# Reordering the joints of a Strassen-style feed-forward on one Trainium2 core: low parts and sums from GpSimd to VectorE, one early eviction, sums and adds at the tail placed anew

## What is computed

```python
x = x + rmsnorm(ox @ p['x_wo'], nrm[3])
h = rmsnorm(x, nrm[4])
u, fconv_new = causal_dwconv(h @ p['f_wu'], fconv, p['f_conv_w'], p['f_conv_b'])
x = x + rmsnorm((jax.nn.gelu(u) * (h @ p['f_wg'])) @ p['f_wd'], nrm[5])
```

## Time and profile before

| | us |
|---|---|
| median of 3 runs | 2322.34 (2321.3 to 2322.55) |
| the profiled execution, its time | 2326.86 |
| its span, first to last instruction | 2325.1 |
| PE busy in it | 2185.2 (94%) |
| DVE busy | 1285.1 (55%) |
| ACT busy | 845.4 (36%) |
| POOL busy | 631.3 (27%) |
| mean granted TensorE clock | 0.964 of full |

### The profile page before, as it was taken

How to read it: one execution, slowest core, us unless ns; L and a number is a source line. 1 busy time by engine, 2 the same in 40 slices (tenths; PEclk the granted TensorE clock), 3 DMA queues, 4 the chain that set the end, 5 groups by cost and what they waited for, 6 DMA issues and landing times. The chain is left out here.

```text
span 2325.1 us, 42807 instructions
## 1 busy us (share of the span) xinstructions
PE 2185.2 (94%) x17107; PEld 2003.3 (86%) x17107; DVE 1285.1 (55%) x2341; ACT 845.4 (36%) x1712; POOL 631.3 (27%) x518
## 2 busy tenths in 40 slices
PE   9999998988888989999899999987899999999996
PEld 7799977865555579999899988987899999999996
DVE  2213354356675761222237154566799887876958
ACT  4221244136655640111243133543333433334353
POOL 0000025502223121211011200235344333445535
PEclk9999999979999999999999999998899999999997
DMA  4211097964444321111310255232223232264243
GB/s 150 99 51 46 28 175 241 326 240 126 147 128 146 125 103 55 59 41 41 129 46 28 98 203 208 95 110 83 88 72 122 84 121 88 84 236 177 90 144 118
DMA packets 133713, 276.33 MB, mean 119 GB/s; under 512 B 24627, under 2 KB 79572, under 8 KB 128333
## 3 DMA queue, kind: packets, MB, share of 16 engines
q1 hardware_dynamic: 110796, 232.32, 30.1%
q0 software_dynamic: 10368, 28.33, 3.7%
q10 hardware_dynamic: 12352, 12.96, 1.7%
HBM read 229.49 MB, written 48.26 MB: 119 GB/s over the span
## 5 line engine op out<-in xcount | busy, mean ns | idle before, releaser
L88 PE MATMUL psum<-merged_high,oq_half 128*128 128x352 f32 x768 | 189.1, 326 | 9.3 <-DVE oq_half L69 7.7
L88 PE MATMUL psum<-ff_t,ff_x_slots 128*128 128x264 f32 x1200 | 149.1, 284 | 0.0
L88 PEld LDWEIGHTS psum<-ff_t,ff_x_slots 128*128 128x128 f32 x1200 | 147.1, 188 | 0.3 <-issue 0.2
L88 PEld LDWEIGHTS psum<-merged_high,oq_half 128*128 128x128 f32 x768 | 135.3, 190 | 9.9 <-DVE oq_half L69 8.0
L1655 POOL DMA_DIRECT2D na_kv<-in_pool x128 | 69.2, 540 | 226.3 <-PE psum L1859 154.9
L88 PE MATMUL psum<-x_half_high,mg_w_high 128*128 128x352 f32 x384 | 124.0, 323 | 2.1 <-ACT gated L2329 1.2
L88 PE MATMUL psum<-h_again_low,mg_w_high 128*128 128x352 f32 x384 | 123.1, 321 | 0.0
L88 PE MATMUL psum<-x_half_high,mg_w_low 128*128 128x352 f32 x384 | 123.1, 320 | 0.0
L1957 ACT ACTIVATE na_pt<-psum 128x512 f32<-128x512 f32 (+1 forms) x170 | 86.4, 543 | 89.1 <-PE psum L1832 80.6
L88 PE MATMUL psum<-ff_bslot,ff_x_slots 128*128 128x264 f32 x888 | 117.5, 285 | 0.0
L88 PEld LDWEIGHTS psum<-ff_bslot,ff_x_slots 128*128 128x128 f32 x888 | 112.4, 189 | 0.1
(11 more groups left out here) (667 smaller groups left out, 5662.9 us busy)
## 6 DMA issues: line engine op xcount, KB each, us to landing
na_kv<-in_pool SPq DMA_DIRECT2D x128, 128.0 KB, 3.8
na_kv<-in_pool POOLq DMA_DIRECT2D x128, 128.0 KB, 4.2
ff_bslot_raw<-mid_ops SPq DMA_DIRECT2D x59, 264.0 KB, 3.2
mid_ops<-ff_bufs SPq DMA_DIRECT2D x11, 1056.0 KB, 3.9
mg_w<-in_w_merge SPq DMA_DIRECT2D x15, 768.0 KB, 4.3
ring<-in_f_wu SPq DMA_DIRECT2D x11, 1024.0 KB, 5.2
low<-in_f_wg SPq DMA_DIRECT2D x22, 512.0 KB, 4.5
first_pages<-in_pool SPq DMA_DIRECT2D x68, 128.0 KB, 6.0
```

Of the source, the lines that this page charges most:

```text
L88: ins = nc.tensor.matmul(out, w[a], x[b], start=first and n == 0, stop=last and n == 2)
```

## The change

- GpSimd keeps the sum `t3,0` and the low part `b22,0`. The low parts `b22,1`, `t1,0`, `t4,0` and the sums `t3,1`, `t4,0` are now DVE's, at given places in its list.
- The eviction c11 of i = 2 comes before the low part `t3,1`; a semaphore of its own (`c11_early`) replaces its count, with `wait_c11` for its readers. u3 of 0 comes before c11 of 1, and the first weight sums of i = 1 before u4 of 0.
- In `pass1`, `spread(0)` moves from after step 2 to after step 1; `sums2(0)` and `(1)` from 8 to 9, `spread2(0)` from 9 to 10, `spread2(1)` from 11 to 12. DVE does `add_square(7, 2)` before the low part `b11,1`, the low part `b21,1` after the first `factor` of the third group, and both `add(3, ..)` before the `mean` of the second norm.
- The eleven differences of down weights for p = 3 are formed while the pieces for p = 4 are prepared.
- In the tail DVE does the residual adds of groups 0 and 1 right after their scales; POOL keeps group 2. `sums3(2)` comes after c = 1, j = 0 and `spread3(2)` after j = 2. DVE scales group 2 before the fourth part of group 3 is added.

The diff without the list of semaphore names (`c11_early` and `summed5` are added there):

```diff
@@ -3216,11 +3216,12 @@
         x_stored = [sem(f"x_stored{g}") for g in range(4)]
-        T_POOL, T_DVE = (("t3", 0), ("t3", 1), ("t4", 0)), (("t1", 0), ("t1", 1), ("t2", 0), ("t2", 1), ("t4", 1))
+        T_POOL, T_DVE = (("t3", 0),), (("t1", 0), ("t1", 1), ("t2", 0), ("t2", 1), ("t3", 1), ("t4", 0), ("t4", 1))
         HIGH_ORDER = [("b11", 0), ("b21", 0), ("b11", 1), ("b21", 1), ("b22", 0), ("t3", 0), ("b22", 1), ("t2", 0), ("t2", 1), ("t3", 1),
                       ("t1", 0), ("t1", 1), ("t4", 0), ("t4", 1)]
-        LOW_POOL = [("b22", 0), ("b22", 1), ("t1", 0), ("t4", 0)]
-        LOW_DVE = [("b11", 0), ("b21", 0), ("b11", 1), ("b21", 1), ("t2", 0), ("t2", 1), ("t3", 0), ("t3", 1), ("t1", 1), ("t4", 1)]
+        LOW_POOL = [("b22", 0)]
+        LOW_DVE = [("b11", 0), ("b21", 0), ("b11", 1), ("b21", 1), ("b22", 1), ("t2", 0), ("t2", 1), ("t3", 0), ("t3", 1), ("t1", 0), ("t1", 1),
+                   ("t4", 0), ("t4", 1)]
         block = ctx.enter_context(nc.Block())
@@ -3270,9 +3271,17 @@
 
+        def wait_c11(eng, i):
+            if i == 2:
+                eng.wait_ge(S["c11_early"], 1)
+            else:
+                eng.wait_ge(S["c11"], i + 1 if i < 2 else i)
+
         def wait_closed(eng, i, p):
...
                 eng.wait_ge(S["p3_kept" if p == 3 else "c22"], 1)
+            elif p == 2:
+                wait_c11(eng, i)
             else:
@@ -3328,7 +3337,7 @@
         WD_SUM = {}
-        for p, per in ((7, 1), (6, 2), (5, 0), (3, 1)):
+        for p, per in ((7, 1), (6, 2), (3, 1), (5, 0)):
             for q in range(KP):
@@ -3447,10 +3456,10 @@
                 for n, f in enumerate((0, 4) if g < 2 else (4, 0)):
-                    if g < 3:
+                    if g < 2:
                         sp.wait_ge(S["summed3"], 2 * g + n + 1)
                     else:
-                        sp.wait_ge(S["summed4"], n + 1)
+                        sp.wait_ge(S["summed5" if g == 2 else "summed4"], n + 1)
                     c = slice(f, f + 4)
@@ -3592,9 +3601,10 @@
                             ins.then_inc(S["z_done"], 1)
-                            if c == 1 and j == 1:
+                            if c == 1 and j == 0:
                                 sums3(2, 2 * down_pairs[0])
-                    spread3(2, 2 * down_pairs[1])
+                            elif c == 1 and j == 2:
+                                spread3(2, 2 * down_pairs[1])
                     return
@@ -3632,16 +3642,16 @@
                     sums(1)
-                elif t == 2:
+                elif t == 1:
                     spread(0)
...
                     spread(1)
-                elif t == 8:
+                elif t == 9:
                     sums2(0)
                     sums2(1)
-                elif t == 9:
+                elif t == 10:
                     spread2(0)
-                elif t == 11:
+                elif t == 12:
                     spread2(1)
@@ -3984,7 +3994,7 @@
                 w = xa[g // 2][:, ks, col(g % 2)]
-                nc.gpsimd.tensor_tensor(w, w, z[:, ks, col(g)], ALU.add).then_inc(S["summed3"], 1)
+                nc.gpsimd.tensor_tensor(w, w, z[:, ks, col(g)], ALU.add).then_inc(S["summed5"], 1)
 
@@ -3993,13 +4003,8 @@
             low_of(6)
-            operand_low("b22", 1)
-            t_sum("t3", 1)
             low_of(9)
             low_of(10)
-            operand_low("t1", 0)
-            t_sum("t4", 0)
-            operand_low("t4", 0)
             for n in range(11, ND):
@@ -4007,9 +4012,6 @@
                     low_of(down_at(pi, q))
-            for g in range(2):
-                for n, f in enumerate((0, 4)):
-                    add3(g, f, n)
             for n, f in enumerate((4, 0)):
@@ -4142,7 +4144,7 @@
                 elif what == "u2":
-                    ve.wait_ge(S["c11"], i + 1)
+                    wait_c11(ve, i)
                     ins = tt(cols(t12), src, cols(t12), ALU.add)
@@ -4162,11 +4164,14 @@
                     ins = tt(cols(t12), src, cols(t12), ALU.add)
-                ins.then_inc(S[what], 1)
+                ins.then_inc(S["c11_early" if (i, what) == (2, "c11") else what], 1)
 
...
                 m, h = int(what[1]) - 1, int(what[2]) - 1
-                ve.wait_ge(S["c" + what[1:]], 2 * q + 2)
+                if what == "m11":
+                    wait_c11(ve, 2 * q + 1)
+                else:
+                    ve.wait_ge(S["c" + what[1:]], 2 * q + 2)
                 ve.wait_ge(S["gelu_ready"], 2 * q + 2)
@@ -4242,8 +4247,7 @@
                 elif p == 3:
-                    wait_low(ve, down_at(DP[6], q))
-                    ve.wait_ge(S["wd12"], 16)
+                    wait_low(ve, down_at(DP[2], q))
                     ve.wait_ge(S["wd_sum"], WD_SUM[(6, q)])
@@ -4295,6 +4299,13 @@
                 nc.vector.tensor_scalar(rstd[0:TW, 2, c], psum[0:TW, at_bank, c], 1.0 / D, EPS, ALU.mult, ALU.add).then_inc(S["mean3_ready"], 1)
+
+            def add3(g, f, n):
+                ks = slice(f, f + 4)
+                ve.wait_ge(S["scaled3"], 2 * g + n + 1)
+                ve.wait_ge(x_again[g // 2], 16)
+                w = xa[g // 2][:, ks, col(g % 2)]
+                tt(w, w, z[:, ks, col(g)], ALU.add).then_inc(S["summed3" if g < 2 else "summed4"], 1)
 
@@ -4340,12 +4351,12 @@
             add_square(6, 2)
+            add_square(7, 2)
             operand_low("b11", 1)
-            operand_low("b21", 1)
-            add_square(7, 2)
             mean(SUM, 0, third, "sum_ready", 3, "mean_ready")
...
             factor(0, third, "root_ready", 2, "rstd_ready")
+            operand_low("b21", 1)
             scale(2)
@@ -4355,10 +4366,10 @@
             scale(3)
+            add(3, 0)
+            add(3, 1)
             mean(SUM2, 1, third, "sum2_ready", 3, "mean2_ready")
-            add(3, 0)
             factor(1, third, "root2_ready", 2, "rstd2_ready")
-            add(3, 1)
             normed(2, range(KD))
@@ -4366,26 +4377,31 @@
             t_sum("t1", 0)
+            operand_low("b22", 1)
             t_sum("t1", 1)
...
             operand_low("t2", 1)
+            t_sum("t3", 1)
             weight_low(0, 7)
             operand_low("t3", 0)
+            evac(2, "c11")
             operand_low("t3", 1)
+            operand_low("t1", 0)
             evac(0, "u2")
             operand_low("t1", 1)
+            t_sum("t4", 0)
             t_sum("t4", 1)
+            operand_low("t4", 0)
             operand_low("t4", 1)
+            evac(0, "u3")
             evac(1, "c11")
-            evac(2, "c11")
-            evac(0, "u3")
+            sums_early(1)
             evac(0, "u4")
...
             evac(0, "c22")
-            sums_early(1)
             evac(0, "c21")
@@ -4442,8 +4458,10 @@
                 for v in ahead:
-                    if DOWN_ORDER[v[0]] in (7, 6, 3):
+                    if DOWN_ORDER[v[0]] in (7, 6):
                         wd_sum(*v)
+                    elif DOWN_ORDER[v[0]] == 4:
+                        wd_sum(DP[3], v[1])
                 for i in range(max(len(ahead), len(drains))):
@@ -4452,18 +4470,23 @@
                 if p == 3 and b + 2 == len(blocks):
+                    ve.wait_ge(S["gained"], 8)
                     for g in range(2):
                         ve.wait_ge(S["row3_copied"], g + 1)
-                        ve.wait_ge(S["gained"], 8)
                         for f in (0, 4):
                             scale3(g, f, row3[:, g, :])
+                    for g in range(2):
+                        for n, f in enumerate((0, 4)):
+                            add3(g, f, n)
             for i in range(3):
                 add_square3(slice(0, HN))
-            def finish(c):
-                for j in range(4):
+            def finish(c, some):
+                for j in some:
                     z_add(3, j, c)
...
                         add_square3(col(c))
+                if 3 not in some:
+                    return
                 add_square3(col(c))
@@ -4472,20 +4495,17 @@
 
-            finish(0)
+            finish(0, range(4))
             factor(2, third, "root3_ready", 2, "rstd3_ready")
-            finish(1)
+            finish(1, range(3))
             scale_last(0, 4)
+            scale_last(0, 0)
+            finish(1, range(3, 4))
             factor(2, fourth, "root3_ready", 3, "rstd3_ready")
-            scale_last(0, 0)
             scale_last(1, 4)
...
             for n, f in enumerate((4, 0)):
-                ks = slice(f, f + 4)
-                ve.wait_ge(S["scaled3"], 7 + n)
-                ve.wait_ge(x_again[1], 16)
-                w = xa[1][:, ks, col(1)]
-                tt(w, w, z[:, ks, col(3)], ALU.add).then_inc(S["summed4"], 1)
+                add3(3, f, n)
 
...
 def build(nc, A, O):
```

4 lines of the change are left out of this document (2 added, 2 removed).

## The result

The changed kernel takes 2312.21 us (median of 9 runs, 2304.42 to 2318.68), the kernel before, on the same chip in the same session, 2325.11 (9 runs, 2321.3 to 2334.93). The ratio is 0.9929, 95% interval 0.991 to 0.9948: 12 to 21 us faster. The forecast of 2300.2 was 12.0 too low, and the time is above the range.

The account below looks back on a forecast made before the run. PE is full in the long products, so gains lie in its waits for DVE and POOL at the joints. 5.0 + 14.5 - 2.0 + 4.6 = 22.1 us off 2322.3 gives 2300.2, range 2294.8 to 2308.3 (some 80%).

Parts of the forecast that it names:

- Joint A: Norm passes, 1512 to 1564 us: earlier spreads and reordered DVE work gain 5.0 us, between 4.0 and 5.7.
- Joint B: Start of gate and up products, 1600 to 1647 us: five operations to DVE, c11 forward, gain 14.5 us (12.0 to 15.3).
- DVE chain: DVE's operations from the end of `normed(3)` to product (1,6), counted at 29.9 us; wrong if over 32.
- Rival 1: All PE waits vanish with nothing late next, B worth 21.3 us; time 2293; chance 4%.
- another length behind (1,6): Sign of being wrong: the stretch from product (1,6) to the down products not the same length as before.
- Joint C: Change of product in the down projection: eleven moved differences of down weights cost 2.0 us, between 0 and 5.0.
- second block: Where p=4 begins: 0.6 us added to the cost for the second block of three differences.
- rival 3: Differences alternate with POOL, fourth product stalls in several blocks, tail returns only 3 us: 2311 (2306 to 2317); chance 13%.
- Joint D: The tail, 2284 us on: residual adds on DVE, quarter sums and scales ahead, gain 4.6 us, between 3.0 and 6.5.
- So 23.0 to 23.5 instead of 21.5: Tail from `sums3(2)` to the end: longer than before's 21.5 us; 23.5 taken.
- I subtract the gain from the median: Step to the forecast time: gain reckoned in the profiled execution (2326.86 us), subtracted from the runs' median of 2322.34.
- Rivals 4 and 5: 4: another wait holds B's chain, about 2320, 5%; 5: DVE bounds the fourth product, half clock, 2324 to 2329, 3%.

Follow-up runs that it names:

- A alone: Kernel before with only the moved spreads and sums2, reordered squares, low part and adds of the norm passes: 2325.23 us, ratio 0.9986.
- C alone: Kernel before with only the eleven differences of down weights moved ahead of p=4: 2335.07 us in one run, beside 2331.85 before.
- D alone: Kernel before with only the tail changed (residual adds on DVE, quarter sums and scales ahead): 2324.01 us in one run, beside 2331.85 before.
- POOL held back: Changed kernel with POOL's group 2 adds after the last square and p=3 differences after the p=6 drains: 2304.77 us, ratio 0.9905.
- second set: The changed kernel again, no edit, against the kernel before: medians 2309.78 (6 runs) and 2327.88 us (23 runs), ratio 0.9922.
- C and D: Kernel before with both the moved differences of down weights and the changed tail: 2334.73 us in one run, beside 2331.85 before.

## Why the prediction was right or wrong

**Joint A, 5.0 (4.0 to 5.7): right.** `scale(0)` was to start 2.95 earlier. It stands 56.05 us into the stage against 60.09 before; 1.1 of those 4.0 is the clock of the first matmuls, since after a start at full clock the unchanged code has it at 58.9: 2.9. `normed(1)` starts 90.97 us into the stage instead of 96.86 (said: 4 us earlier). The tree's wait is gone, PE waits 2.68 at `sums(2)` ("about 3"), and DVE is what it waits for. `sums(2)` comes 7.1 us earlier than in the profile of before and 4.9 to 5.6 earlier than in the four executions of old code that began at full clock (101.45 to 102.15). With A alone (1,6) is 5.7 earlier than in before, 4.6 without the first 1.1. But by then the clock counts for more than A does: (1,6) stands 181.30 us into the stage with A alone, and 181.56 and 180.89 with C alone and D alone, which leave A's code as it was. The medians give A 0.2 to 6 us.

**Joint B, 14.5 (12.0 to 15.3): right, with one gain not seen.** At equal clock it is 14.57. The forecast's DVE chain was 29.9 us from the end of `normed(3)` to (1,6). The timeline of after:

```profile
1603.35 0.70 DVE L4145 TENSOR_TENSOR ff_bufs<-psum,ff_bufs 128x528 f32<-128x528 f32 x1
...
1611.80 3.15 PE L88 MATMUL psum<-ff_t,ff_slot_e 128*128 128x264 f32 x24 [1.08 <-DVE ff_t L69]
...
1616.43 6.12 PE L88 MATMUL psum<-ff_t,ff_slot_e 128*128 128x264 f32 x48 [1.48 <-DVE ff_bufs L4145]
...
1624.23 3.16 PE L88 MATMUL psum<-ff_t,ff_slot 128*128 128x264 f32 x24 [1.68 <-DVE ff_t L69]
...
1632.96 1.29 DVE L69 TENSOR_TENSOR ff_slot<-ff_slot_raw,ff_slot 128x512 fp32r<-128x512 f32 x2
...
1633.80 8.15 PE L88 MATMUL psum<-ff_t,ff_slot 128*128 128x264 f32 x48 [6.42 <-DVE ff_slot L69]
```

From 1603.35 to 1633.80 it is 30.45, with waits of 1.08, 1.48, 1.68 and 6.42 (said: 1.4, 1.9, 1.9 and 5). (1,6) stands 166.74 us into the stage, 20.2 earlier (said: 19.5, A and B together), and 19.1 without the 1.1 of the first matmuls. Rival 1, that all waits vanish, is out by the same row. What the forecast denied is the 2.0 us in stretch c: "after (1,6) the orders are the same", but DVE comes to the next products with less behind it, and two small waits there, 1.47 and 1.09, become one of 0.5. The forecast had named another length behind (1,6) as a sign of being wrong, and it came.

**Joint C, −2.0 (0 to −5.0): −2.7.** The term was 0.9 for each difference, less idle time, plus a second block. They took 1.73 each, and no second block stalled. 0.9 was drawn as a mean where the row has two prices and nothing between: of the eleven in the trace of before, eight take 0.68 to 0.69 us and three 1.78 to 1.80, and each of these three starts while a low part of POOL is under way, none of the eight does. The four that took 4.72 us together are two of either kind. So the bound from the earlier trace rows, 1.80, was the price to take beside a POOL that has work queued. The Trainium skill, "SBUF — State Buffer", section "Who interferes with whom", which has a VectorE operation with two SBUF inputs and a GpSimd operation that reads SBUF shut each other out, agrees with this row: 1.73 where 0.62 is the free price, and 0.70 as before for sums that read PSUM. Several blocks stalled, as rival 3 has it, did not come: d is 494.83 to 494.89 wherever the first three are away from the drains.

**Joint D, +4.6 (3.0 to 6.5): +1.7, the term that failed.** `sums3(2)` came 5.9 earlier in its stretch (said: 6.6); the four scales took 5.85 us (said: 4.9), the four adds 4.75 (4.9). PE waited 4.21 there (said: 2 to 4). The miss is behind it. "So 23.0 to 23.5 instead of 21.5" was 25.7: the working followed PE and DVE, and has no term for POOL's two adds of the third quarter. But `scale(2)`, moved ahead of the last squares, sets them free just there, and two squares took 3.92 us instead of 1.00. With POOL held back it is 22.7, a little better than said. The rule of the Trainium skill named at C bears on this place too, and the trace agrees with it; it had been weighed for C and B, and not for D.

**The sum inside the stage** is right by chance more than by its terms: 22.1 said, 21.3 measured. By stretches, 0.7 more than said up to (1,6) (0.4 less without the first matmuls' 1.1), 2.0 more in c, 0.7 less at C, 2.9 less at D. C and D together were to bring 2.6 and lost 1.0.

**The step that failed for the time** is "I subtract the gain from the median" of 2322.34. That was a median of three runs within 1.25 us of each other, and I took their closeness for its certainty. Nine runs of the same kernel span 13.6 us with a median of 2325.11, and all 44 on record have one of 2327.87: the base was 2.8 us too low by the first and 5.5 by the second. Of the 12.0 us by which the forecast was low, 2.8 are this base in the first set, 0.8 are the stage's sum, and 8.4 are left, since the medians of the first set differ by 12.9 and not by the profiled stage's 21.3.

Part of these 8.4 can be told from the record. The medians of the first set are themselves uncertain: the interval of its ratio ends at 20.9 us, the second set's medians differ by 18.1, those of all runs by 17.3. The profiled before was also at the slow end of its own code: (1,6) stands 186.98, 186.87, 186.46, 181.56 and 180.89 us into the stage in the five executions with a and b unedited (mean 184.6), and 166.74, 166.71, 166.78 and 161.97 in the four with those of the changed kernel (mean 165.6), so A and B are worth 19.0 there and not 20.2. The rest, how the first set's two medians came to be only 12.9 us apart, is open: what the unprofiled runs did in each stage is in no trace. From the median of all 44 runs the same gain gives 2305.8 and a range of 2300.4 to 2313.9, which holds the time; from the first set's 2325.11 the range ends at 2311.1, which does not. That the base was too low is thus shown; its share of the miss is not settled.

The range had the bounds of the four terms and nothing for the spread of starts of untouched stages, 1458.87 to 1472.64, or for a stretch b that differs by up to 6 us with the clock at the same code (78.87 to 85.01). With 4 us more at its upper end it would have held the time, and the profiled starts alone span 14.

The time lies where rival 3 was placed (2306 to 2317), but that is luck of the number. Of its conditions the first three differences did alternate with POOL, at 1.73 us, and D returned less than 3; but the fourth product stalled in one place alone, for 2.7 us in all and not 11 to 12, and the stage got 21.3 us shorter where the rival had 11. Rivals 4 and 5 did not occur.

## What to carry to other kernels

When a change lies in one stage, cut the trace at rows that both kernels have, and compare stretches; whole times of single runs, and even medians of few, carry the luck of all the other stages, and a range has to have a term for it. Whoever moves an operation on one engine should also ask whom it sets free: a scale moved ahead of two squares released POOL's adds onto them. In a count for an engine that shares with POOL, ask of each operation with both operands in SBUF what POOL runs beside it, and price it by the single operations beside which POOL did so, and not by a mean over a group that mixes two prices.

## What was not expected of the hardware

- DVE and POOL do not hold each other in one way. In joint B, DVE back to back let one POOL operation of 2.44 us wait until it had taken 11.07; in the down projection the two alternate one for one, 1.73 and 1.71 us each; in the tail two DVE squares take 3.92 us instead of 1.00 while two POOL adds take 4.97 instead of 4.78. What decides between these was not tried.
- The same wait of 2.68 us on PE is followed by half clock in one execution (0.67 over 10 us) and full clock in another (1.00), with all code around it the same; this is worth 4.5 us (b 70.20 and 65.71). The two groups of 48 single-column products of `sums_early` take from 3.85 us (D alone, clock 1.00) to 7.10 (C and D, clock 0.50) with the same code. In before the clock is 1.00 for 3 us ahead of the first group and 0.77 over its 4.85 us, with PE busy throughout: it also falls where PE has no idle time. Whether these products are the reason no run tells.
- Executions of the same instructions reach 1460 us with a spread of 14 us, and the stage behind that, where its clock went the same way, repeats to 0.1 us (865.50 and 865.40; 844.24 and 844.20).
